# A hybrid decoder layer on one core: the input projection as seven block products per unit in four token passes

## What is computed

```python
h = rmsnorm(x, norm_g)                       # (tokens, 1024)
z = jnp.einsum('btd,de->bte', h, w_in)       # D_IN = 3460 columns
q_a, k_att, v_a, f_a, g_a, sh_b, g_b, u_c, g_c, u_d, g_d = split_cols(z)
o_a = attend(qh, kh, vh, logf)               # forgetting attention, 4 heads x 64
o_b, wkv1, shift1 = rwkv7_mix(sh_b, ...)     # token shift, decay, matrix state
o_c, pool1 = pool_mixer(u_c, ...)            # causal pooling, windows 2/4/8/16
o_d, conv1 = conv_module(u_d, ...)           # GLU, depthwise width 31, LayerNorm, swish, pointwise
mixed = jnp.concatenate([o_a * silu(g_a), o_b * silu(g_b), o_c * silu(g_c), o_d * silu(g_d)], axis=-1)
x = x + jnp.einsum('bte,ed->btd', mixed, w_out)
```

## Time and profile before

| | us |
|---|---|
| median of 3 runs | 1674.02 (1671.11 to 1678.54) |
| the profiled execution: span from first to last instruction | 1668.8 |
| the median less that span | 5.2 |
| PE busy | 1612.8 (97%) |
| VectorE busy | 806.7 (48%) |
| ScalarE busy | 487.3 (29%) |
| GpSimd busy | 127.0 (8%) |

### The profile page before, as it was taken

How to read it: one execution, slowest core, us unless ns; L and a number is a source line. 1 busy time by engine, 2 the same in 40 slices (tenths; PEclk the granted TensorE clock), 3 DMA queues, 4 the chain that set the end, 5 groups by cost and what they waited for, 6 DMA issues and landing times.

```text
span 1668.8 us, 32594 instructions
## 1 busy us (share of the span) xinstructions
PE 1612.8 (97%) x13510; PEld 967.5 (58%) x13510; DVE 806.7 (48%) x1782; ACT 487.3 (29%) x946; POOL 127.0 (8%) x166
## 2 busy tenths in 40 slices
PE   6999999999999999999999999999899999999998
PEld 3555555555555555558745666668788764444443
DVE  5560199974212234533066676644454549343333
ACT  5301100001106352410245565553233353010001
POOL 1100000002100000000000000000000003222220
PEclk9999999999999999999999999999999999999999
DMA  7232332137541315581266546567676559999983
GB/s 264 73 132 98 119 106 72 66 120 192 171 129 64 142 38 217 198 292 63 88 181 191 149 137 185 179 201 224 190 217 183 182 192 361 353 332 352 356 321 130
DMA packets 150797, 302.87 MB, mean 181 GB/s; under 512 B 16725, under 2 KB 121381, under 8 KB 132278
## 3 DMA queue, kind: packets, MB, share of 16 engines
q1 hardware_dynamic: 128714, 155.65, 29.8%
q0 software_dynamic: 17280, 117.18, 19.7%
q10 hardware_dynamic: 4656, 27.96, 4.1%
HBM read 237.88 MB, written 65.10 MB: 182 GB/s over the span
## 4 chain that ended last, share of the span: by engine, by line
PE 78%; DVE 12%; ACT 4%; DMA 4%; issue 2%; SPq 1%; ACTq 0%; DVEq 0%
PE psum L875 29%; PE psum L1134 24%; DVE big L1901 9%; PE psum L846 5%; PE psum L956 4%; PE psum L1094 4%; PE psum L1012 4%; PE psum L1080 3%; PE psum L901 2%; PE psum L1439 2%; ACT big L1557 2%; DMA pars<-zT 1%; DMA big<-in_xT 1%; PE psum L1342 1%; PE psum L943 1%
## 5 line engine op out<-in xcount | busy, mean ns | idle before, releaser
L875 PE MATMUL psum<-big,wbuf 128*128 128x416 f32 x1920 | 677.7, 514 | 12.2 <-DVE big L1807 10.8
L875 PEld LDWEIGHTS psum<-big,wbuf 128*128 128x128 f32 x1920 | 365.3, 191 | 318.6 <-issue 313.4
L1134 PE MATMUL psum<-big 64*64 64x64 f32 (+4 forms) x5440 | 256.0, 269 | 14.1 <-issue 7.4
L1134 PEld LDWEIGHTS psum<-big 64*64 64x64 f32 (+2 forms) x5440 | 176.9, 132 | 99.3 <-issue 73.3
L1530 ACT ACTIVATE zst<-psum 128x416 f32<-128x416 f32 x123 | 63.0, 517 | 522.4 <-PE psum L875 522.3
L1901 DVE SCALAR_TENSOR_TENSOR big<-big,pars 128x2048 f32<-128x2048 f32 x120 | 148.2, 1298 | 1.1
L746 POOL DMA_INDIRECT big<-in_cache_v,pidx x64 | 69.7, 1090 | 682.7 <-PE psum L1094 468.5
L846 PE MATMUL psum<-ident,big 128*128 128x128 f32 (+1 forms) x556 | 78.7, 280 | 7.5 <-ACT big L1711 3.3
L1080 PE MATMUL psum<-wbuf,big 128*64 128x128 f32 x544 | 77.0, 281 | 0.6 <-ACT big L1680 0.3
L1080 PE MATMUL psum<-big 128*64 128x128 f32 x544 | 77.0, 282 | 0.0
L846 PEld LDWEIGHTS psum<-ident,big 128*128 128x128 f32 (+1 forms) x556 | 61.2, 145 | 26.5 <-issue 13.1
(11 more groups left out here) (311 smaller groups left out, 1690.0 us busy)
## 6 DMA issues: line engine op xcount, KB each, us to landing
big<-in_k_pages SPq DMA_DIRECT2D x432, 128.0 KB, 2.3
zT<-zst ACTq DMA_DIRECT2D x25, 1040.0 KB, 6.1
wbuf<-in_w_slots SPq DMA_DIRECT2D x24, 512.0 KB, 4.1
big<-zT POOLq DMA_DIRECT2D x11, 1024.0 KB, 5.6
zst<-in_k_pages SPq DMA_DIRECT2D x80, 128.0 KB, 2.7
rwS<-big POOLq DMA_DIRECT2D x8, 1024.0 KB, 4.2
big<-rwS SPq DMA_DIRECT2D x8, 1024.0 KB, 5.7
out_y_prompt<-big SPq DMA_DIRECT2D x16, 512.0 KB
```

Source lines behind the costliest of these rows:

```text
L875: last = nc.tensor.matmul(psum[:, m % CHUNKS, 0:CW], w[:, k, :], x, start=(k == 0), stop=(k == KT - 1))
L1134: return nc.tensor.matmul(out, l, r, start=start, stop=stop, skip_group_check=True)
```

## The change

**Seven products.** The weights are taken in 12 *units* of two neighbouring slots, 256 columns. The unit's product, 256 columns by 1024 rows by a pass of tokens, is a 2 x 2 block product (the rows halved, the columns halved, the tokens of the pass halved), and is made of seven block products instead of eight, in Winograd's form: each product is 4 matmuls of 128 x 128 by half a pass. The seven need sums of blocks: four of the weights (`weight_sums`, on GpSimd, per unit), and four of the tokens (`token_sums`, on VectorE, per pass). The products go to banks 0, 1, 2, again 0, 1, 2 (accumulated on what stands there), and 3. ScalarE copies each of the first six out (`copies`), VectorE makes the four output blocks of the six copies and adds the seventh straight from bank 3 (`evac`).

**Four passes.** The tokens go in four passes of 512 (the first with the 32 samples, so 544; half a pass is 256 or 272 columns), and all 12 units are run in each pass, so each unit's 1 MB of weights is read and summed four times. The 25th slot (`WA`, the low-rank inputs) stays a plain product of 8 matmuls by 2 halves in each pass, and the value rows of a pass stand at its start.

**The mixers' row work** is done pass by pass in SBUF from the rows as VectorE writes them, with small carried edges (`halos`), and no longer goes through `zT`; only four pairs of rows (keys, queries, two gates) are still stored there. `TAPS` tells how many of the 31 taps follow each unit, `MEAN_AT` and `VAR_AT` where the convolution's mean and variance stand. The small matmuls rotate through banks 4 to 7.

**Around attention's start.** The convolution's last product (`conv_out(3)`) and item 0's scores stand behind all units. `decode_queries` and the first two `forget_sums` move behind items 3, 4 and 7, and the 4 MB copy into `scores_` is issued after `conv_out(3)` has been read.

```diff
+PASSES, PT_W, UNITS = 4, 512, 12
+WID = (PT_W + SMP, PT_W, PT_W, PT_W)
+U_C, U_U1, U_U2, U_R, U_K, U_V, U_GD, U_GC, U_KA, U_QA, U_GA, U_GB = range(UNITS)
+        TAPS = ((0, 0, 5, 4, 4, 4, 6, 8), (0, 0, 5, 4, 4, 4, 6, 8), (0, 0, 5, 4, 4, 4, 6, 8), (0, 0, 2, 2, 5, 5, 8, 9))
+        MEAN_AT, VAR_AT = (8, 8, 8, 9), (10, 10, 10, 11)
...
+            def weight_sums(U):
+                u = U % 2
+                w, s = w_pair[u], w_sums[u]
+                pool.wait_ge(w_in[u], 16 * (U // 2 + 1))
+                if U >= 2:
+                    pool.wait_ge(prod, 7 * (U - 1))
+                g.tensor_tensor(s[0], w[:, 1, 0:4, :], w[:, 1, 4:8, :], ALU.add).then_inc(sums_ready, 1)
+                g.tensor_tensor(s[1], w[:, 0, 0:4, :], w[:, 1, 0:4, :], ALU.subtract).then_inc(sums_ready, 1)
+                pool.wait_ge(sums_ready, 4 * U + 2)
+                g.tensor_tensor(w[:, 1, 0:4, :], s[0], w[:, 0, 0:4, :], ALU.subtract).then_inc(sums_ready, 1)
+                pool.wait_ge(sums_ready, 4 * U + 3)
+                g.tensor_tensor(s[2], w[:, 0, 4:8, :], w[:, 1, 0:4, :], ALU.subtract).then_inc(sums_ready, 1)
...
+            def product(p, i, j, bank, left, right, first=True):
+                U = UNITS * p + i
+                if j < 3:
+                    if U >= 1:
+                        pe.wait_ge(z_cp, 6 * U - 2 + j)
+                elif j < 6:
+                    pe.wait_ge(z_cp, 6 * U + j - 2)
+                elif U >= 1:
+                    pe.wait_ge(z_add, adds_through((U - 1) // UNITS, (U - 1) % UNITS))
+                for k in range(4):
+                    last = nc.tensor.matmul(psum[:, bank, 0:wide(p) // 2], left(k), right(k), start=first and k == 0, stop=k == 3, skip_group_check=True)
+                last.then_inc(prod, 1)
...
+            def copies(p, i, first, last):
+                U = UNITS * p + i
+                n = wide(p) // 2
+                for j in range(first, last):
+                    if j == 0 and U >= 2:
+                        act.wait_ge(z_add, adds_through((U - 2) // UNITS, (U - 2) % UNITS))
+                    act.wait_ge(prod, 7 * U + j + 1)
+                    nc.scalar.activation(parts_[:, U % 2, j, 0:n], psum[:, (0, 1, 2, 0, 1, 2)[j], 0:n], ACT.Copy, scale=0.125 if i == U_QA else 1.0).then_inc(z_cp, 1)
...
+            def evac(p, i):
...
+                v.tensor_tensor(s[:, M5], s[:, M5], s[:, M7], ALU.add).then_inc(z_add, 1)
...
+                total(0, 1, s[:, U2_], s[:, X_])
+                dve.wait_ge(z_cp, 6 * U + 6)
+                total(1, 0, s[:, U2_], s[:, Y_])
+                dve.wait_ge(z_add, done)
+                total(1, 1, s[:, U2_], s[:, M5])
+                dve.wait_ge(prod, 7 * U + 7)
...
+                    total(0, 0, s[:, M1], psum[:, 3, 0:n])
...
+            def bank_of(g):
...
+                if emitted[0] >= 4:
+                    pe.wait_ge(*read_sem(SMALL[emitted[0] - 4]))
...
-            dve.wait_ge(a_in, 64)
-            decode_queries()
-            forget_sums(0)
-            forget_sums(1)
+            dve.wait_ge(wkv_stored, 16)
+            dve.wait_ge(rw_stored, 64 * PASSES)
             dve.wait_ge(ck_in[0], 16)
...
+                    if j == 3:
+                        dve.wait_ge(a_in, 64)
+                        dve.wait_ge(out_stored, 16 * 6)
+                        decode_queries()
+                    if j in (4, 7):
+                        forget_sums(j // 5)
```

1793 lines of the change are left out of this document (1039 added, 754 removed).

## The result

The changed kernel takes **1746.0 us** (median of 4 runs, 1740.1 to 1750.4) against 1673.4 for the kernel before on the same chip: ratio **1.042** (95% interval 1.039 to 1.045), 4.2% slower. The forecast was 1645 with a range up to 1697, so the time lies above the range, and the kernel became slower where it was to become faster.

The account below looks back on a forecast made before the run. TensorE, busy for 97% of the span, was taken as the bound. The terms -74.4 + 3 + 9 + 11 + 2 + 2 + 5 + 14 = -28.4 gave a 1640.4 us span, 1645 us forecast; range 1604 to 1697.

Parts of the forecast that it names:

- GpSimd term: Projection: GpSimd's weight sums make VectorE stand still, taken as 0.65 us per sum: +14 us, bounds 0 and 84.
- 2.1 us a unit to spare: Units 2 to 7, passes 1 and 2: VectorE needs 67.5 us against TensorE's 80, leaving 12.5 us spare.
- rival B: VectorE becomes the bound in units 2 to 7 of every pass: 84 us instead of 14, 1715 us; chance 0.15.
- 2 us for the clock: Gap before attention: about 10 us of idle lowers TensorE's clock again, +2 us (0 to 4).
- matmuls removed: Projection: seven products for eight cut TensorE's matmul records from 705.8 to 631.4 us, 74.4 us less.
- pass 3's waits: TensorE waits 5.3 us after unit 9 and 3.8 after unit 10 of pass 3: together +9 us (4 to 12).
- The start: Up to the value rows: TensorE idle for about 14 us, as before; change 0, between -2 and +5 us.
- the 815 of the prediction: End of the projection: the last product was to come before 815 us if the forecast was right.
- The mean's waits: Pass 0, unit 8: the convolution's mean waits for all taps because VectorE is late, +3 us (0 to 8).
- the 765 of the prediction: Projection: TensorE was to be busy for near 765 us if the forecast was right.
- From the projection into attention: Last product to item 0's first transposes: 16.9 us, with TensorE working 5.8 of them, +11 us (6 to 16).
- First items of attention: Query copy and scans in items 3 to 7, +2 us; loads behind the 4 MB into `scores_`, +5 (0 to 15).

Follow-up runs that it names:

- e7: Changed kernel with the transfers around attention's start reordered (masks earlier, prefixes after conv's store, 4 MB copy at item 2): ratio 1.0367 to the kernel before.

## Why the prediction was wrong

- **The sum's GpSimd term failed: +14 us, and 73.4 came.** The standstill per sum was taken as 0.65 us and measures 0.77. The error was in what it costs. I had given VectorE 2.1 us a unit to spare, 0.52 us per sum free; scaled from there, 0.25 above the free 0.52 would be 27 us (as 0.13 gave 14) to 40 (as rival B's 0.52 gave 84). But nothing was free: copies with 0.22 us of standstill cost 15.1 us. Even without any sums TensorE waits for the taps before the mean in each of the passes 0 to 2, 9.9 us in all, where the 12.5 us to spare should have left no wait in passes 1 and 2: the 2.1 us existed only as an average over six units, and the instructions that TensorE waits for pay from the first stall on. And idle time of TensorE came back a second time as a lower clock, 20.6 us, for which the sum had nothing (its 2 us for the clock stand for the gap before attention).
- **Rival B was the right mechanism; that its price came near is luck.** It had 20 us a pass, 28 in pass 0, 16 in pass 3, against 18.7 and 17.9, 25.1 and 11.7. But it needed 1.04 us per sum for that, and by its own rule 0.77 would have given the 40 above: a standstill too long and a price too low made up for each other. Its sign, waits in most units of passes 1 and 2, didn't come either: there are four waits of over 1 us in each, of 2.6 to 6.8. I gave it 0.15.
- **Right: the matmuls removed, and the places of pass 3's waits.** The products cost 0.218 us a record in passes 1 and 2, for 0.221, and without sums the two waits come at 5.2 and 2.7 us where 5.3 and 3.8 were worked out. The start is within its bounds (17.1 us idle before 45, for 14). The seventh product's bank itself was hardly waited for: 9.2 us for line 2092 in the whole projection.
- **The rest of the projection: 23 us more than the sum had, with no sums at all.** By the terms without the 14, and with 5.3 us of TensorE's small groups moved behind it, the last product was due at 855.9 - 74.4 + 3 + 9 - 5.3 = 788 us; without sums it came at 811.1. That it lies before the 815 of the prediction shows little, since those had room for the sums. TensorE is idle for 45.0 us instead of 28.6. The mean's waits took 9.9 for 3, and three waits were taken as nothing: 3.3 for the key norms of pass 0, 2.8 for ScalarE in pass 3, 2.5 for its copies; the start has 4.5 more than before. In return the 2.8 us of waits that the kernel before had are gone. And it is busy for 766.1 us instead of 759.6, at a granted clock of 0.98: that this is near the 765 of the prediction is luck, as the moved groups and the clock about cancel.
- **From the projection into attention: +11 and +2, and 16.5 came.** The 21.8 us by which the gap grew hold the 5.3 us of moved work as well; TensorE's idle time in it grew by 12.6, and the work took 3.9 more at a granted clock of 0.66. The first transposes were due 16.9 us after the last product and came at 23.0. The chain was worked out to the end of PE's four groups at 13.3 us; they ended at 14.7. What I left out is that VectorE's next step waits for all small constants, and the masks land 20.4 us after the last product behind a 5 us round trip of the prefix rows. e7 got 5.3 us of it back.
- **First items of attention: +2 and +5, 24.3 came.** Here the mechanism was named (loads queued behind 4 MB) and its price, 5 of 0 to 15, was too low by more than the bounds allowed. Before, the 4 MB had landed 13 us ahead of the last product (VectorE's scan over them starts at 842.8). Now they land behind it, because products, weights and sums hold those areas to the end. I checked each transfer against its own deadline, not the bytes together against the rate. How much of the 17 us above the two terms is bytes and how much the order of waits in SP's queue stays open.
- Together: 59 us for the sums, 23 in the rest of the projection, 3.5 in the gap and 17 behind it are the 103 us between the forecast and the measured span.
- Without the sums the kernel is level with before (0.9988), not at the 1631 of my sum. Its last product is 44.8 us earlier than before's, and the gap and the stretch behind it cost 48.3 us more. Either of the two losses alone takes the gain: with the sums the last product comes 28.6 us later than before's.

## What to carry to other kernels

Before GpSimd gets full-tile arithmetic beside a busy VectorE, count it as VectorE's work: here 0.77 us of VectorE for 1.3 us of GpSimd, worse than the 0.69 us of doing it on VectorE at a place of one's choice. Spare time averaged over a stretch is not slack; look for the waits TensorE already has on that engine. And when a change keeps memory in use until the last instruction of a phase, add up the bytes that must land behind it: four orders gave 4 to 9 us of the stretch and each moved the wait, 4 MB fewer gave 9.3, and a first use three items later 7.5 more.

## Not expected of the hardware

A GpSimd sum of 512 columns that starts during VectorE's taps can last 4.33 us (5.58 the longest of 192, shortest 1.26), so both sides lose. Twenty-four copies of 2 columns on VectorE took 0.54 us in the mean, and 0.17 in the same places without the sums. A GpSimd copy (0.60 us) stops VectorE for 0.22 us in the mean, a sum (1.26) for 0.77, a memset for 0.01. From the recurrence on, profiled executions with the same instructions differ by up to 13 us (540.8 to 554.0, the kernel before 550.9); none of the experiments was about that, it stays open, and differences of a few us between whole times can come from there.
